# Seven places instead of six in a weight ring, with gate rows loaded as column blocks

## What is computed

```
mod = c_act @ ada_w[layer] + ada_b[layer]
shift_t, scale_t, gate_t, shift_m, scale_m, gate_m = split(mod, 6)
h = modulate(rms_norm(x, norm_g[layer, 0]), shift_t, scale_t)
x = x + gate_t[:, None, :] * mixer(h)
h = modulate(rms_norm(x, norm_g[layer, 1]), shift_m, scale_m)
x = x + gate_m[:, None, :] * (square(relu(h @ w1)) @ w2)
```

## Time and profile before

| | |
|---|---|
| median of 3 runs | 2391.28 us (2390.61 to 2391.47) |
| the profiled execution | 2394.44 us, span 2392.7 us |
| TensorE matmul | busy 2344.7 us, 98% |
| VectorE | busy 1794.8 us, 75% |
| ScalarE | busy 1260.1 us, 53% |
| DMA | 665.36 MB, 278 GB/s in the mean |
| granted TensorE clock | 0.998 of full speed |

### The profile page before, as it was taken

One profiled execution on the slowest core, in us unless ns is written; L12 is line 12 of the kernel. 1 busy time (PEld: TensorE's weight loads), 2 busy tenths in 40 slices (PEclk: granted clock), 3 DMA queues, 4 the chain that ended last, 5 costly groups with the idle time before them and its releaser, 6 DMA issues.

```text
span 2392.7 us, 28882 instructions
## 1 busy us (share of the span) xinstructions
PE 2344.7 (98%) x11309; PEld 1934.7 (81%) x11309; DVE 1794.8 (75%) x2333; ACT 1260.1 (53%) x2148; POOL 35.6 (1%) x66
## 2 busy tenths in 40 slices
PE   8999999999999999999999999999999999999999
PEld 4468888877878888888887878878788888888887
DVE  6677888878989888888787888769875555555554
ACT  3165566557534544634547676654653553553552
POOL 1000000001000000000001000000100000000000
PEclk9999999999999999999999999999999999999999
DMA  9987878956999989888895886747875555555555
GB/s 392 425 322 278 311 290 307 357 198 245 375 369 353 335 298 340 297 332 331 295 368 207 326 306 251 278 171 286 291 298 194 191 188 193 191 188 193 192 187 173
DMA packets 150999, 665.36 MB, mean 278 GB/s; under 512 B 17392, under 2 KB 17872, under 8 KB 121424
## 3 DMA queue, kind: packets, MB, share of 16 engines
q1 hardware_dynamic: 150864, 663.53, 75.7%
HBM read 661.33 MB, written 2.13 MB: 277 GB/s over the span
## 4 chain that ended last, share of the span: by engine, by line
PE 79%; DVE 7%; DMA 7%; ACT 5%; issue 1%; SPq 0%; ACTq 0%; DVEq 0%
PE main L512 18%; PE main L426 14%; PE main L428 14%; PE main L427 14%; PE main L514 9%; DMA w_raw<-w 3%; DMA qT<-ada 3%; DVE w_lo L1307 2%; DVE ada_raw L1314 2%; PE main L440 2%; PE main L442 2%; PE main L441 2%; ACT w_hi L887 1%; DMA ada_raw<-ada 1%; ACT st_a L927 1%
## 5 line engine op out<-in xcount | busy, mean ns | idle before, releaser
L887 ACT ACTIVATE w_hi<-w_raw 128x1024 fp32r<-128x1024 f32 x771 | 810.3, 1058 | 796.0 <-DMA w_raw<-w 792.0
L1307 DVE TENSOR_TENSOR w_lo<-w_raw,w_hi 128x1024 fp32r<-128x1024 f32 x771 | 934.0, 1223 | 378.5 <-ACT w_hi L887 372.6
L1314 DVE CUSTOM_DVE_ANT_0 ada_raw<-ada_raw,c_row,biasc 128x2048 f32<-128x2048 f32 x208 | 492.1, 2366 | 47.9 <-DMA ada_raw<-ada 45.5
L512 PE MATMUL main<-hT,w_hi 128*128 128x512 f32 x1856 | 464.7, 392 | 0.0
L512 PEld LDWEIGHTS main<-hT,w_hi 128*128 128x128 f32 x1856 | 334.3, 189 | 60.1
L426 PE MATMUL main<-w_hi,mid_hi 128*128 128x512 f32 x960 | 374.0, 390 | 1.9 <-DVE w_lo L1307 1.9
L427 PE MATMUL main<-w_lo,mid_hi 128*128 128x512 f32 x960 | 373.5, 389 | 0.0
L428 PE MATMUL main<-w_hi,mid_lo 128*128 128x512 f32 x960 | 373.5, 389 | 0.0
L426 PE MATMUL main<-w_hi,hT 128*128 128x512 f32 x848 | 341.1, 402 | 0.0
L428 PE MATMUL main<-w_hi,hT 128*128 128x512 f32 x848 | 330.9, 390 | 0.0
L427 PE MATMUL main<-w_lo,hT 128*128 128x512 f32 x848 | 330.0, 389 | 0.0
(11 more groups left out here) (263 smaller groups left out, 1768.9 us busy)
## 6 DMA issues: line engine op xcount, KB each, us to landing
w_raw<-w SPq DMA_DIRECT2D x800, 512.0 KB, 4.2
ada_raw<-ada SPq DMA_DIRECT2D x208, 1024.0 KB, 7.0
qT<-ada SPq DMA_DIRECT2D x16, 1024.0 KB, 12.3
gate<-gate_rows SPq DMA_DIRECT2D x4, 1024.0 KB, 7.2
xs<-x SPq DMA_DIRECT2D x1, 2048.0 KB, 7.6
out<-xs SPq DMA_DIRECT2D x3, 512.0 KB, 6.1
out<-xs SPq DMA_DIRECT2D x2, 256.0 KB, 2.5
st_a<-lamb SPq DMA_DIRECT2D x1, 256.0 KB, 17.7
```

The source lines that it names most:

```text
L512: pe.matmul(banks[f][:, :], w_hi[:, s, wc], hT[:, :, kt, :], start=(kt == 0), stop=False)
L887: act.activation(w_hi[:, s, :], w_raw[:, s, :], ACT.Copy).then_inc(hi_done, 1)
L1307: dve.tensor_tensor(w_lo[:, s, :], w_raw[:, s, :], w_hi[:, s, :].bitcast(F32), ALU.subtract).then_inc(lo_done, 1)
L1314: dve.tensor_tensor_reduce(piece, piece, c_row[:, :], gain, biasc[:, section, kt:kt + 1], ALU.mult, ALU.add, out).then_inc(ada_used, 1)
```

## The change

SLOTS is 7. Each place of the ring costs 8 KB per partition (4 for `w_raw` with `w_lo`, 4 for `w_hi`). Room comes from `gate`, which holds two blocks of 512 columns and not four (4 KB less), from an unused tile `ones` and its memset on GpSimd, and from smaller pads. A gate block c now lies in place c % 2. `gate_load` loads one block of 256 KB when the update that used its place is done (x_done), with a semaphore for each place; every update and every `leave` of tile 0 waits for its block. There are 40 such loads in place of four of 1 MB: each of the 40 updates has its own. In the MLPs they stand in SyncE's queue behind piece 3 of chunks 5, 6, 7 and 8 of each block of eight (blocks 2, 3, then 0 and 1 for the next round). `turn` moves to the second block. TensorE's first wait is for one constant and not two.

```diff
-SLOTS = 6
+SLOTS = 7
...
-        gate = sb("gate", [P, 4, NC])
+        gate = sb("gate", [P, 2, NC])
...
-        ones = sb("ones", [P, P])
...
-        turn = gate[:, 2, 0:T * P].rearrange("p (t n) -> p t n", t=T)
+        turn = gate[:, 1, 0:T * P].rearrange("p (t n) -> p t n", t=T)
...
-            def gate_read(g, updates):
-
-                sp.wait_ge(gate_out, 64 * (g + 1))
-                if updates:
-                    sp.wait_ge(x_done, updates)
-                sp.dma_start(gate_flat, gate_rows[g].partition_broadcast(P)).then_inc(gate_in, 16)
+            def gate_load(g, c):
+
+                updates = n["gate"].n
+                n["gate"].up()
+                if c == 0:
+                    sp.wait_ge(gate_out, 64 * (g + 1))
+                if updates >= 2:
+                    sp.wait_ge(x_done, updates - 1)
+                sp.dma_start(gate[:, c % 2, :], gate_rows[g, cols(c, NC)].partition_broadcast(P)).then_inc(gate_in[c % 2], 16)
+
+            def first_gates(g):
+
+                gate_load(g, 0)
+                gate_load(g, 1)
+
+            def block_gates(ch, g):
+
+                if ch % 8 == 0:
+                    return {3: lambda: gate_load(g, 1)} if ch else {}
+                c = {5: 2, 6: 3, 7: 0}.get(ch % 8)
+                return {} if c is None else {3: lambda: gate_load(g, c)}
...
-            gate_steps = {0: {3: lambda: gate_write(0)}, 1: {2: lambda: gate_read(0, 0)}}
+            gate_steps = {0: {3: lambda: gate_write(0)}, 1: {2: lambda: first_gates(0)}, 3: {3: lambda: gate_load(0, 2)}}
...
-            chunk(0)
-            gate_steps = {3: {5: lambda: gate_write(1), 7: lambda: gate_read(1, 4)}}
+            chunk(0, then={1: lambda: gate_load(0, 3)})
+            gate_steps = {3: {5: lambda: gate_write(1), 7: lambda: first_gates(1)}}
             for ch in range(8):
-                chunk(ch, ada=ADA_GATE + ADA_FIRST, then=gate_steps.get(ch, {}))
+                chunk(ch, ada=ADA_GATE + ADA_FIRST, then=gate_steps.get(ch, block_gates(ch, 1)))
             for ch in range(8 + 8 + 7):
-                chunk(ch, ada=ADA_MLP)
+                chunk(ch, ada=ADA_MLP, then=block_gates(8 + ch, 1))
...
-            gate_steps = {2: {3: lambda: gate_write(2), 6: lambda: gate_read(2, 4 + 16)}}
+            gate_steps = {2: {3: lambda: gate_write(2), 6: lambda: first_gates(2)},
+                          11: {3: lambda: gate_load(2, 2), 4: lambda: gate_load(2, 3)}}
...
                     if t == 0:
                         dve.wait_ge(tile_done, n["tile"].up())
+                        dve.wait_ge(gate_in[1], 16 * n["gate1"].up())
...
-                    scaled_y = dve.tensor_tensor(sta[:, t, :], main[1][t][:, :], gate[:, 3, :], ALU.mult)
+                    scaled_y = dve.tensor_tensor(sta[:, t, :], main[1][t][:, :], gate[:, 1, :], ALU.mult)
...
-            def update(c, back=4, fresh=False):
+            def update(c, back=4):
...
-                    if fresh:
-                        dve.wait_ge(gate_in, n["gate"].up(16))
+                    dve.wait_ge(gate_in[c % 2], 16 * n[f"gate{c % 2}"].up())
...
-            pool.memset(ones[:, :], 1.0).then_inc(consts, 1)
```

More of the change, by code:

```diff
@@ L148, in sem @@
             return sems[name]
-        sb("pad", [P, 96])
         with nc.sbuf_tensor("w_lo", [P, SLOTS, PK * NC], F32R) as w_lo:
@@ L215, in trunk @@
         pos_i = sb("pos_i", [P, T], I32)
-        sb("skip", [P, 192])
+        sb("skip", [P, 32])
         with nc.sbuf_tensor("mid_hi", [P, KT, T * P], F32R) as mid_hi, \
@@ L262, in trunk @@
         c_ready, c_wide, c_spread = sem("c_ready"), sem("c_wide"), sem("c_spread")
-        gate_col, gate_turn, gate_out, gate_in = sem("gate_col"), sem("gate_turn"), sem("gate_out"), sem("gate_in")
+        gate_col, gate_turn, gate_out = sem("gate_col"), sem("gate_turn"), sem("gate_out")
+        gate_in = [sem(f"gate_in{p}") for p in range(2)]
         read_out = [sem(f"read_out{p}") for p in range(2)]
@@ L380, in _ @@
             chunk(0)
-            gate_steps = {3: {1: lambda: gate_write(3), 4: lambda: gate_read(3, 4 + 16 + 4)}}
+            gate_steps = {3: {1: lambda: gate_write(3), 4: lambda: first_gates(3)}}
             for ch in range(8):
[L383 to L388, removed]
+                chunk(ch, ada=ADA_GATE_B, then=gate_steps.get(ch, block_gates(ch, 3)))
+            for ch in range(8 + 8 + 7):
+                chunk(ch, then=block_gates(8 + ch, 3))
             rows = out.rearrange("(t p) d -> p t d", p=P)
@@ L686, in _ @@
             pe.sem_inc(mm_done, SLOTS)
-            pe.wait_ge(consts, 2)
+            pe.wait_ge(consts, 1)
             pe.wait_ge(vec_in, 16)
@@ L1602, in ended @@
                 dve.wait_ge(mm_done, n["w"].n + SLOTS - back)
-            def update(c, back=4, fresh=False):
+            def update(c, back=4):
                 def step():
                     ended(back)
-                    if fresh:
-                        dve.wait_ge(gate_in, n["gate"].up(16))
+                    dve.wait_ge(gate_in[c % 2], 16 * n[f"gate{c % 2}"].up())
                     settled()
                     for t in range(T):
-                        last = dve.tensor_tensor(stb[:, t, :], main[c % 2][t][:, :], gate[:, c, :], ALU.mult)
+                        last = dve.tensor_tensor(stb[:, t, :], main[c % 2][t][:, :], gate[:, c % 2, :], ALU.mult)
                     last.then_inc(read_out[c % 2], 1)
@@ L1747, in group @@
                     qkv_chunk(5, {4: [sc4[0]], 5: [sc4[1]], 6: [sc4[2]], 7: [sc4[3]], 8: [running_max(1)]})
-            dve.wait_ge(consts, 4)
+            dve.wait_ge(consts, 3)
             dve.wait_ge(gain_in, 16 * 3)
@@ L1764, in _ @@
                                    2: [lows[2], merge(1, 1, False), merged], 4: [lows[3]]})
-            chunk(2, PIECES // 2, {2: [update(0, 3, fresh=True)], 4: [update(1)]})
+            chunk(2, PIECES // 2, {2: [update(0, 3)], 4: [update(1)]})
             chunk(3, PIECES // 2, {4: [update(2)]}, ADA_WO)
@@ L1813, in block @@
                     sides += [{2: [mid_turned(6)], 4: [sum_turned(i, 7)], 6: [mid_turned(7)]}]
-                    sides += [{4: [update(c, fresh=first and c == 0)]} for c in range(3)]
+                    sides += [{4: [update(c)]} for c in range(3)]
                     for c in range(7):
@@ L1854, in _ @@
             section_chunk(9, {1: [sub_norm(6)], 2: [sub_norm(7)], 4: [lows[6]], 5: [lows[7]]})
-            section_chunk(10, {2: [update(0, fresh=True)], 4: [update(1)]})
+            section_chunk(10, {2: [update(0)], 4: [update(1)]})
             section_chunk(11, {4: [update(2)]})
```

## The result

The changed kernel takes 2409.48 us (median of 4 runs, 2407.77 to 2411.53) against 2391.12 us (4 runs, 2390.61 to 2391.47): ratio 1.0067, 95% interval 1.0055 to 1.0079. The forecast was 2385.7 us, its range 2380.0 to 2391.0. The kernel is 18.4 us slower where I expected it 5.5 us faster. The profiled execution took 2407.77 us with a span of 2406.0, so 13.3 us more than the span of before.

What follows compares the result with a forecast made beforehand. The prediction took the kernel as bound by TensorE with small holes. Seventh place 6.1 us won, less 0.3 for gate blocks and 0.3 for the rest, made 5.5 us: median 2385.7 us, range 2380.0 to 2391.0.

Steps and rivals of the forecast that it cites:

- C: Remaining edits: VectorE's 36 more waits cost 0.3 us (bounds 0 and 2); ones memset, smaller pads and turn's new place cost 0.
- A: Seventh ring place: 2.72 us more lead where SyncE waited for a released place, closing TensorE holes; 6.1 us won in all.
- The slower rival: Gate blocks crowd weights in the first layer's MLP, 0.65 us for each of 16, 10.4 us: 2396.2 us; chance 0.06.
- The start: First 133 us, DMA full: one wait on L1366 behind a late weight shrinks; 0.6 us won, between 0 and 1.3.
- The scores: TensorE's waits on masked scores, 5.3 us: late weights delay ScalarE's statistics; 2.0 us won, bounds 0.7 and 5.3.
- The stretch at 676 us: Low halves late behind a slow ada tile and the 1 MB gate row: 1.2 us won, bounds 0 and 1.9.
- The arrivals: Between sublayers: 1.0 us won at 1262.22, 0.6 at 554.94, third arrival 0; sum 1.6, bounds 1.0 and 1.7.
- The hole at 1386.72: 2.58 us hole behind ScalarE, overloaded in one chunk; more lead wins 0.7 us, bounds 0 and 2.6.
- The signs that I named for A: ScalarE's weight-load waits fall, holes at 455, 554, 676, 1272 us shrink, SyncE waits more for dots, less for TensorE.
- Everything behind a late weight goes: Rival: all upper bounds of the seventh place's terms are won, 12.8 us, giving 2378.5 us; chance 0.10.
- The seventh place stays empty where it matters: Rival: ada buffers hold SyncE before nearly every late load; only 1.7 us won, 2389.6 us; chance 0.32.
- B: Gate blocks: 40 loads of 256 KB, 6.3 MB more, mostly covered; 0.3 us lost in the last attention output.

Runs made afterwards that it cites:

- e11: Repeat of e1 (changed kernel, vec allocated ahead of the ring), beside e12 on one chip: 2391.36 us, ratio 0.9990 to the kernel before.
- e1: Changed kernel with the 384-byte tile vec allocated ahead of the ring, which starts again at a multiple of 512 bytes: 2390.14 us, ratio 0.9983 to the kernel before.
- e8: e1 with six places and unused gaps keeping all addresses, so gate blocks alone against the kernel before: 2397.24 us, ratio 1.0014.
- e12: Repeat of e8 (six places, gate blocks, agreeing operands), beside e11 on one chip: 2396.15 us, ratio 1.0013 to the kernel before.
- e3: Kernel before with a longer skip, so mid lies at 191.5 KiB as in the changed kernel: 2395.27 us, ratio 1.0001.
- e10: Kernel before with mid moved 256 bytes on (skip of 256): 2394.30 us in a single run.
- e6: Kernel before without its pad and with skip of 320, so ring, hT and mid are all 128 bytes off: 2399.58 us in one run.
- e2: Kernel before without the pad ahead of the ring, skip longer by as much so mid stays: 2413.03 us, ratio 1.0076.
- e4: Changed kernel with six places and 4 KB gaps keeping all addresses: 2411.71 us, ratio 1.0071 to the kernel before.
- e7: Kernel before with mid alone moved 128 bytes on (skip of 224): 2412.67 us in a single run.
- e9: Kernel before with mid moved 64 bytes on (skip of 208): 2410.85 us in a single run, against 2393.12 for the kernel before.
- e5: Kernel before with its pad moved behind the ring, so the ring alone is 128 bytes off: 2421.22 us in a single run, against 2393.23.

## Why the prediction was wrong

**The failed step** is in C: "Smaller pads and the new place of turn: 0." `turn` was free. The pads were not filler: they held the start of the ring, and with it the moving operand, on the same 256 byte boundary as `mid`. That sentence should have been a term of the sum, 3072 x 5.7 ns = 17.5 us, three times all that A promised. In a kernel in which TensorE is busy 98% of the time, anything that touches its operands, even their addresses, had to be asked about before any stall. The trace of before couldn't have given the price, since the operands of all its 512 column matmuls agree. But the diff showed two pads cut by different amounts, 384 and 640 bytes. That called for a term of its own, "price unknown, at 11,309 matmuls", and for a rival, and the prediction has neither. The slower rival (gate blocks crowd the weights) had the right sign by luck: the changed kernel has no hole between 700 and 1260 us, and where the operands agree the blocks cost 3 us and not 10.4, at most 1.4 of it there. And none of the signs that I had named for being wrong appeared. They were all about loads and holes, and the error was in neither.

The account closes only within the noise. 17.5 us lost less the 2.4 to 4.1 us that e11 and e1 win is 13.4 to 15.1. The spans of the two profiled executions differ by 13.3, the medians by 18.4, with an interval of 13.2 to 18.9.

**A, the seventh place: mechanism right, sum about right, the parts only in part.** 6.1 us were forecast; e1 against e8 gives 0.31% = 7.4 us, e11 against e12 0.23% = 5.5 us, each give or take 3. In the traces TensorE's waits add up to 41.0 and 43.3 us with six places (e8, e12) and to 38.3 and 38.6 with seven (e1, e11), so 2.7 and 4.7 us of it are seen as holes. Term by term, against the timeline of the changed kernel:

```profile
455.13 0.49 PE L586 MATMUL sc<-kT,qT 128*128 128x128 f32 x2 [0.81 <-DVE m L1398]
...
554.32 0.63 PE L471 MATMUL tr<-ident,st_x 128*128 128x128 f32 x4 [0.41 <-DVE st_x L1550]
...
1389.86 1.09 PE L575 MATMUL tr<-ident,st_a 128*128 128x128 f32 x8 [1.80 <-DVE st_a L1378]
```

One trace against one other mixes the seventh place with the gate blocks and with chance. So here are TensorE's waits in us with six places (before; then e8 and e12, which have gate blocks) and with seven (after, e1, e11):

| place | forecast | before | e8, e12 | after, e1, e11 |
|---|---|---|---|---|
| start: the wait on `st_a` at 149 us | 0.6 won | 1.3 | 1.3, 1.3 | 1.7, 1.7, 1.7 |
| scores, all | 2.0 won | 5.3 | 5.3, 5.4 | 4.1, 4.1, 4.5 |
| low halves, 660 to 760 us | 1.2 won | 1.9 | 1.6, 1.6 | 0, 0.4, 0.4 |
| first arrival, 540 to 600 us | 0.6 won | 3.4 | 3.0, 3.1 | 3.1, 3.0, 3.0 |
| second arrival, the hole at 1272.73 | 1.0 won | 1.0 | 0, 1.0 | 0, 0, 0 |
| the hole at 1386.72 | 0.7 won | 2.6 | 0.4, 1.0 | 1.8, 0, 0.3 |
| third arrival, 1655 to 1800 us | 0 | 3.4 | 4.9, 5.2 | 5.0, 4.8, 4.5 |

- *The start*: not won; the wait is longer by 0.4 us in all three kernels with seven places.
- *The scores*: 1.2 us won (5.3 to 4.1, nine waits to six), and not 2.0. The hole at 455 us that I had picked is 0.81 in the changed kernel, gone in e1 and 0.23 in e11: a single hole is a poor example, as it changes between executions.
- *The stretch at 676 us*: the 1.2 us forecast, and won by the place, not by the smaller gate load: with gate blocks and six places 1.6 us are left.
- *The arrivals*: the hole at 1272.73 is gone with seven places each time (and once with six). In the first arrival the holes at 554.94 and 557.96 went from 0.66 and 0.57 to 0.41 and 0.15, but the next one, which I had said would stay, grew from 0.75 to 1.19, and e8 and e12 show the same without the seventh place. So 1.0 of the 1.6 came.
- *The hole at 1386.72*: open. It is 2.58 us before and 1.80 after, but 3.02 in e3 and 1.04 in e10, which are the old kernel with `mid` elsewhere.

The signs that I named for A hold. ScalarE's and VectorE's splitting, after:

```profile
L899 ACT ACTIVATE w_hi<-w_raw 128x1024 fp32r<-128x1024 f32 x771 | 803.8, 1057 | 653.6 <-DMA w_raw<-w 650.3
L1319 DVE TENSOR_TENSOR w_lo<-w_raw,w_hi 128x1024 fp32r<-128x1024 f32 x771 | 929.7, 1223 | 278.0 <-ACT w_hi L899 274.3
```

ScalarE stood 796.0 us before for weight loads and its line, VectorE 378.5. And SyncE's queue, to be read against the earlier trace rows:

```profile
SPq L300 <- PE main L440: 865.2, 385, 5.3
...
SPq L306 <- DVE modc L1326: 149.0, 40, 9.5
...
SPq L306 <- DVE gate_cols L1326: 81.1, 34, 7.7
```

It waits less for TensorE (977.8 before) and more for dots (89.0 and 37.5 before): with seven places the two ada buffers become what stops it more often. One of my rivals is settled by this: "Everything behind a late weight goes", 12.8, is out. "The seventh place stays empty where it matters" gave a gain of 1.7 in all; e1 and e11 have 0.17% and 0.10%, 4.1 and 2.4 us, between it and the forecast's 5.5, and their intervals (1.7 to 6.5 and 0.2 to 4.5 us) leave it possible.

**B, the gate blocks: undersized.** Forecast 0.3 us, bounds 0 and 1.3; measured 0.13 to 0.14%, 3.2 us. SyncE never waits for x_done at a gate load and VectorE never for a block, as forecast. A block lands in 5.4 us, the whole row took 7.2:

```profile
w_raw<-w SPq DMA_DIRECT2D x800, 512.0 KB, 4.4
ada_raw<-ada SPq DMA_DIRECT2D x208, 1024.0 KB, 7.2
gate<-gate_rows SPq DMA_DIRECT2D x40, 256.0 KB, 5.4
```

I had taken 2.5 us for 256 KB from the output's stores, which run when nothing else does; among the weights it is over twice that. The weight loads went from 4.2 to 4.4 us, but they take 4.3 in e8 and e12 and in most of the old kernel's other traces, so that is not the blocks' doing. The term that was too small is the one for the last attention output: I gave its two blocks "up to 1.3 us, I take 0.3", and the third arrival behind it waits 1.5 to 1.8 us more (e8, e12). The place that I had called the tightest, the first attention output, shows nothing of the kind. The Trainium skill, DMA: Bandwidth & Descriptors, Rules for kernel authors, asks for 1 MiB and more per DMA where bandwidth is wanted. The rows agree in direction: a quarter of the bytes took 5.4 us where the whole took 7.2. But 40 such loads did not come near the 10.4 us of the rival that I hung on it.

**The rest of C.** The waits that VectorE got more of: no row of them shows. They may be part of B's 3.2 us.

**Together**: with operands that agree, the change as it was meant is worth 0.10 to 0.17%, 2.4 to 4.1 us of the forecast 5.5. That is just about what a measurement of this kernel can tell. The pads turned it into 18 us lost. e1 is the version that beats both kernels: 0.9983 and 0.9990 in two batches, with one line of the changed kernel moved.

## What to carry to other kernels

When an edit moves a tile in SBUF, list the start addresses of the operands of the hot matmuls before and after, and keep the stationary and the moving one at the same place modulo 256 bytes (as far as tried here: fp32r, 512 columns); a pad that nothing reads may be there for just that. In a kernel bound by TensorE, look first at the mean of one matmul and at its step, operand pair by operand pair, and only then at waits: here the waits got better while the time got worse. To price a small DMA, take a row of one among the same traffic, not of one that runs alone.

## What the runs showed of the hardware

A matmul of a 128x128 stationary block with 512 moving fp32r columns starts every 226.7 ns in a chain of such at the full clock. That is with the activations stationary, in `gemm`. When the start of one operand differs from that of the other by 64 or 128 bytes modulo 256, it is 233.3 or 232.4 ns, 2.5 to 2.9% more; with a difference of 0 or 256 bytes it is 226.7.

| kernel | ring | hT | mid | step of mid matmuls | mean mid, hT |
|---|---|---|---|---|---|
| before | 0 | 0 | 0 | 226.7 ns | 389, 390 |
| e3 (mid 2560 bytes on) | 0 | 0 | 0 | 226.7 | 389, 391 |
| e10 | 0 | 0 | 256 | 226.7 | 389, 390 |
| e6 | 128 | 128 | 128 | 226.7 | 389, 391 |
| after, e2, e4 | 128 | 128 | 0 | 232.2 to 232.5 | 395, 390 |
| e7 | 0 | 0 | 128 | 232.4 | 395, 391 |
| e9 | 0 | 0 | 64 | 233.3 | 395, 390 |
| e5 | 128 | 0 | 0 | 232.3 | 395, 395 |

It is the relative place that counts: absolute ones are on both sides of the table. The cost comes with either operand stationary, but not the same: in e5 a matmul with stationary `hT` pays 4.7 ns, one with the weights stationary (L512, whose moving operand is two runs of 256 columns) 2.7: eight of them in a row take 1.84 us before and 1.86 to 1.87 in e5. Which of these two differences makes it less was not tried. The weight loads of TensorE for the mid matmuls last 188 ns in both kernels, so the rows don't show the cost there. The 256 column matmuls (L514) showed nothing. Why the chip does this the runs don't say; differences under 64 bytes and of 192, and other types, were not tried. e5, e6, e7, e9 and e10 rest on one execution each.
